# Preparation of the time-mixing operands placed beside the second half of the projection

## The reference, cut to what matters

```python
n = rms_norm(x, ln1_g)
proj = n @ w_in                          # 1024 -> 3072 columns
rkv = centred_conv(proj[..., :1536], conv_rkv)
r, k, v = split(rkv)                     # 512 each
# low-rank layer of the time mixing
delta = 0.5 * (shift_prev(n) + shift_next(n)) - n
g = sigmoid((n + delta * mix_g) @ gate_g1) @ gate_g2
kk = normalise(k * k_k)                  # per head of 64
for d in range(2):
    w = exp(-DECAY * sigmoid(decay_w0[d] + tanh((n + delta * mix_w[d]) @ decay_w1[d]) @ decay_w2[d]))
    a = sigmoid(aaa_a0[d] + ((n + delta * mix_a[d]) @ aaa_a1[d]) @ aaa_a2[d])
    kd = k * (1 + (a - 1) * k_a)
    y += wkv7_scan(r, w, kd, v, -kk, kk * a, reverse=(d == 1))
    bonus += sum(r * kd * r_k) * v
```

## Time and profile before

| | us |
|---|---|
| median of 3 runs | 2380.55 (2373.26 to 2381.06) |
| profiled execution, its own time | 2381.69 |
| its span, first to last instruction | 2379.9 |
| mean granted TensorE clock | 0.934 of full |
| TensorE busy | 2144.3 (90%) |
| VectorE busy | 1139.2 (48%) |
| ScalarE busy | 841.2 (35%) |
| GpSimd busy | 418.8 (18%) |

### The profile page before, as it was taken

The page is one execution under the profiler, slowest core; times in us unless marked ns, Lnnn a source line. Parts: engine busy times, 40 slices in busy tenths (PEclk is TensorE's granted clock), DMA queues, the critical chain, the costliest instruction groups (busy, mean ns, idle before and its releaser), DMA issues. The chain is left out here.

```text
span 2379.9 us, 41105 instructions
## 1 busy us (share of the span) xinstructions
PE 2144.3 (90%) x16892; PEld 1803.2 (76%) x16892; DVE 1139.2 (48%) x1613; ACT 841.2 (35%) x1445; POOL 418.8 (18%) x440
## 2 busy tenths in 40 slices
PE   6999999875567888778999799999999999999999
PEld 5887667643445555577886588999998899999887
DVE  5436553289685766655778543232333132323222
ACT  6213553366463444453454222222222122222211
POOL 0002331000006995064454000000000000000000
PEclk8999999867777999958999899999999999999999
DMA  4222111545871001048882644222233332222231
GB/s 159 95 88 81 41 61 61 188 182 218 297 208 57 1 1 54 12 121 183 188 185 71 200 140 147 88 71 79 71 102 94 122 115 79 72 78 71 80 124 67
DMA packets 134064, 258.96 MB, mean 109 GB/s; under 512 B 11200, under 2 KB 81216, under 8 KB 132512
## 3 DMA queue, kind: packets, MB, share of 16 engines
q1 hardware_dynamic: 133920, 256.93, 34.8%
HBM read 184.98 MB, written 68.93 MB: 107 GB/s over the span
## 5 line engine op out<-in xcount | busy, mean ns | idle before, releaser
L224 PE MATMUL ff_acc<-normed_nh,normed_ff_low 128*128 128x320 f32 x1344 | 416.5, 310 | 6.5 <-SPq L172 5.3
L225 PE MATMUL ff_acc<-normed_nl,normed_ff_high 128*128 128x320 f32 x1344 | 416.2, 310 | 0.0
L226 PE MATMUL ff_acc<-normed_nh,normed_ff_high 128*128 128x320 f32 x1344 | 416.1, 310 | 0.0
L2796 DVE TENSOR_TENSOR normed_ff_low<-normed_ff_raw,normed_ff_high 128x1024 fp32r<-128x1024 f32 x126 | 154.4, 1225 | 427.8 <-ACT normed_ff_high L2760 427.6
L224 PEld LDWEIGHTS ff_acc<-normed_nh,normed_ff_low 128*128 128x128 f32 x1344 | 253.2, 188 | 7.2 <-SPq L172 5.6
L225 PEld LDWEIGHTS ff_acc<-normed_nl,normed_ff_high 128*128 128x128 f32 x1344 | 253.2, 188 | 0.0
L226 PEld LDWEIGHTS ff_acc<-normed_nh,normed_ff_high 128*128 128x128 f32 x1344 | 253.2, 188 | 0.0
L2760 ACT CAST normed_ff_high<-normed_ff_raw 128x1024 fp32r<-128x1024 f32 x126 | 131.8, 1046 | 234.7 <-PE ff_acc L226 233.8
L225 PE MATMUL ff_acc<-normed_ff_low,ff_hh 128*128 128x512 f32 x420 | 163.4, 389 | 0.0
L224 PE MATMUL ff_acc<-normed_ff_high,ff_hl 128*128 128x512 f32 x420 | 163.4, 389 | 0.0
L226 PE MATMUL ff_acc<-normed_ff_high,ff_hh 128*128 128x512 f32 x420 | 163.4, 389 | 0.0
(11 more groups left out here) (343 smaller groups left out, 4377.8 us busy)
## 6 DMA issues: line engine op xcount, KB each, us to landing
ch_ops<-dram_sx SPq DMA_DIRECT2D x88, 256.0 KB, 5.3
normed_ff_raw<-in_w_gate SPq DMA_DIRECT2D x44, 512.0 KB, 3.5
normed_ff_raw<-in_w_up SPq DMA_DIRECT2D x44, 512.0 KB
normed_ff_raw<-in_w_down SPq DMA_DIRECT2D x44, 512.0 KB, 3.7
dram_sx<-pr_sx SPq DMA_DIRECT2D x7, 2816.0 KB, 8.1
pj_packed<-in_w_in SPq DMA_DIRECT2D x24, 512.0 KB, 4.6
heads_vt<-dram_sx SPq DMA_DIRECT2D x44, 256.0 KB, 4.9
dram_proj<-pj_mixed SPq DMA_DIRECT2D x12, 656.0 KB, 3.5
```

Of the source, the lines that this page charges most:

```text
L224: nc.tensor.matmul(out, ll, rh, start=start, stop=False)
L225: nc.tensor.matmul(out, lh, rl, start=False, stop=False)
L226: return nc.tensor.matmul(out, lh, rh, start=False, stop=stop)
L2796: nc.vector.tensor_tensor(low[s][:, :], raw[s], high[s][:, :].bitcast(F32), ALU.subtract).then_inc(cut_low[s], 1)
```

## The change

The two Blocks become one, norm_project_prep.

- The tiles of the projection come in another order (ORDER): k, r and v of f = 0, then of f = 1, and so on, then the attention's tiles.
- The 24 low-rank items stand behind pieces 6 to 31 (piece_of), beside the tiles that are convolved, where they stood behind pieces 36 to 62.
- From piece 36 on the projection uses three PSUM banks; the fourth and those of the low-rank layer go to the preparation.
- The preparation goes by 12 units (four f, three ranges of 512, 512 and 384 padded tokens), one each 2.75 pieces from piece 36: its first decays behind piece w0_at, the second ones and VectorE's whole unit at the next piece, the second exponentials at the one after.
- A unit's sx and bonus are stored, and the k, r and v of the unit three further on are loaded, from within SyncE's loop over the pieces. A tile's weights are loaded one tile earlier.
- The buffers of the preparation lie where those of the first half lay. So piece 33 brings a hand-over: hidg is stored, GpSimd waits for that and clears the padding, then the first loads are issued.
- The nine loads for the next Block go into the place of nh and nl, so they are issued only after the last piece.
- The next Block waits for the projection's stores itself.

```diff
-def norm_project_lora(nc, g):
+def norm_project_prep(nc, g):
+    ORDER = [n * FT + f for f in range(FT) for n in (1, 0, 2)] + list(range(CONV, MT))
-    BANKS = 4
+    BANKS, LATER_BANKS, CHANGE = 4, 3, PIECES // 2
-    chunk_of = lambda item: TN * CONV + item + item // KT
+    piece_of = lambda item: FIRST + item + item // KT
+    START, RATE = CHANGE, 2.75
+    w0_at = {START + int(RATE * u): u for u in range(NU)}
+    w1_at = {i + 1: u for i, u in w0_at.items()}
+    exp_at = {i + 2: u for i, u in w0_at.items()}
+    LOADS_AT = piece_of(ALL_ITEMS - 1) + 2
...
             @block.sync
+                load(2)
+                for i in range(PIECES):
+                    if i in finished:
+                        p = finished[i]
+                        if p + 3 < MT:
+                            load(p + 3)
+                        store(p)
+                    if i == LOADS_AT:
...
+                        sp.dma_start(g.hidg_dram[:, 0, :], hidg[:, 0, :]).then_inc(hidg_stored, 16)
+                        sp.dma_start(g.hidg_dram[0:GL - P, 1, :], hidg[0:GL - P, 1, :]).then_inc(hidg_stored, 16)
+                        sp.wait_ge(padded, 1)
...
+                        for u in range(len(SEGS)):
+                            load_kr(u)
+                            load_v(u)
+                    if i in exp_at:
+                        u = exp_at[i]
+                        store_sx(u, 0)
+                        if u:
+                            store_bonus(u - 1)
+                            if u + 2 < NU:
+                                load_v(u + 2)
+                        store_sx(u, 1)
+                        if u + 3 < NU:
+                            if UNITS_OF[u + 3][1] == 0:
+                                rows_stored(UNITS_OF[u + 3][0])
+                            load_kr(u + 3)
+                sp.wait_ge(done, PIECES)
+                for to, of in ((g.raw_first, g.proj[CONV * P:(CONV + 1) * P, :]), (g.cos_sb, g.cos), (g.sin_sb, g.sin),
+                               *((t, g.small_of(name)) for name, t in g.ahead_small.items())):
+                    sp.dma_start(to[:, :], of).then_inc(ahead_in, 16)
...
             @block.tensor
+                    if u or d:
+                        pe.wait_ge(sig_w, 2 * u + d)
+                        pe.wait_ge(sig_a, 2 * u + d)
+                    for ps, rows, sem in ((psw, HALVES[0], w_prod), (psa, HALVES[1], a_prod)):
+                        nc.tensor.matmul(span(ps, u), w2[rows, f, d, :], g.hid[rows, d, in_seg(u)], start=True, stop=True).then_inc(sem, 1)
...
+                    if i in w0_at:
+                        u = w0_at[i]
+                        decays(u, 0)
+                        if u == 0:
+                            pe.wait_ge(heads_in, 48)
+                            square_sums(0)
+                        else:
+                            bonus_of(u - 1)
+                    if i in w1_at:
+                        u = w1_at[i]
+                        decays(u, 1)
+                        spread_norms(u)
+                        if u + 1 < NU:
+                            square_sums(u + 1)
...
             @block.scalar
+                    if i in exp_at:
+                        u = exp_at[i]
+                        exponentials(u, 1)
+                        if u + 1 < NU:
+                            root_k(u + 1)
+                        if u + 2 < NU:
+                            square_k(u + 2)
+                        if u + 1 < NU:
+                            to_rows(u + 1)
+                    if i == START - 1:
+                        square_k(0)
+                    if i in w0_at:
+                        u = w0_at[i]
+                        sigmoids(u, 0)
...
+                    if i in w1_at:
+                        u = w1_at[i]
+                        sigmoids(u, 1)
+                        scale_a(u, 0)
+                        scale_a(u, 1)
+                        exponentials(u, 0)
...
             @block.vector
+                def unit(u):
+                    s = UNITS_OF[u][1]
+                    sums_of(u, 0)
+                    sums_of(u, 1)
+                    if u:
+                        bonus_of(u - 1)
+                    to_come(u)
+                    norm_k(u)
...
+                    if u + 1 < NU:
+                        floor(u + 1)
+                    operands(u, 0)
+                    if u + 1 < NU:
+                        invert_k(u + 1)
+                    operands(u, 1)
...
+                    if i in w1_at:
+                        unit(w1_at[i])
-def prep(nc, g):
...
@@ def solve_and_attention_in
                 sp.dma_start(heads[:, :], g.small_of("quarter_heads")).then_inc(small_in, 16)
+                for sem in g.proj_stored:
+                    sp.wait_ge(sem, g.proj_stores)
                 load_raw(1)
```

More of the change, by code:

```diff
@@ L258, in norm_project_lora @@
[L258 to L263, removed]
+        with Ctx(nc, "lo") as early:
+            own = early.sb("own", (P, 4, D))
+            lw, lwg = early.sb("w", (P, KT * 4 * HD)), early.sb("wg", (P, KT * GL))
+            less, half = (early.sb(n, (P, 5 * KT)) for n in ("less", "half"))
+            nk = [early.sb(f"nk{s}", (P, 514)) for s in range(2)]
+            near = [early.sb(f"near{s}", (P, 512)) for s in range(2)]
+            hidg = early.sb("hidg", (P, 2, PTOK))
+            partial, fold = early.sb("partial", (P, 512)), early.sb("fold", (P, BLK))
+            gate_mix = [early.sb(f"gate_mix{s}", (P, 512)) for s in range(4)]
+            ss, mean, rms, rstd = (early.sb(n, (P, TT)) for n in ("ss", "mean", "rms", "rstd"))
+            mixed = [early.sb(f"mixed{s}", (P, TOK)) for s in range(2)]
@@ new lines, in norm_project_prep @@
+        late = c.enter_context(Ctx(nc, "pr"))
+        slots = lambda name: [late.sb(f"{name}{s}", (P, 512)) for s in range(2)]
+        k, r, v = ([late.sb(f"{n}{s}", (P, hi - lo)) for s, (lo, hi) in enumerate(SEGS)] for n in ("k", "r", "v"))
+        w2, first = late.sb("w2", (P, FT, 2, P)), late.sb("first", (P, 512))
+        heads_rk, without_a = late.sb("heads_rk", (P, FT, P)), late.sb("without_a", (P, FT))
+        q, rows, kk, kds, bon = (late.sb(n, (P, 512)) for n in ("q", "rows", "kk", "kds", "bon"))
@@ new lines, in norm_project_prep @@
+        sg, av, cs, ex, kd = (slots(n) for n in ("sg", "av", "cs", "ex", "kd"))
+        tot, st = late.sb("tot", (P, 2, 512 // CH)), late.sb("st", (P, 2, 2 * 512 // P))
+        sx = [late.sb(f"sx{d}", (P, 512 // CH, 4, CH)) for d in range(2)]
+        with Ctx(nc, "parts") as parts:
+            g.nh, g.nl = (parts.sb(n, (P, KT, TT * P), F32R) for n in ("nh", "nl"))
+        g.lend_ahead(nc)
+        pair_mix = [own[:, :, :].rearrange("p s d -> p (s d)")[:, s * 512:(s + 1) * 512] for s in range(8)]
@@ new lines, in load_v, with rows_stored @@
+                def load_v(u):
+                    f, s = UNITS_OF[u]
+                    if f:
+                        sp.wait_ge(bonus, u - len(SEGS) + 1)
+                    row = (2 * FT + f) * P
+                    for at, token, n_tok in runs_of[s]:
+                        sp.dma_start(v[s][:, at:at + n_tok], g.proj[row:row + P, token:token + n_tok]).then_inc(v_in[s], 16)
+                def rows_stored(f):
+                    for p in range(3 * f + 1, 3 * f + 3):
+                        sp.wait_ge(stored[p % 2], 16 * (p // 2 + 1))
@@ L458, in _ @@
                 turn(10)
-                for i in range(3, len(SEQUENCE)):
+                for i in range(3, PIECES):
                     product(i)
@@ L2864, in __init__, with lend_ahead @@
         self.keep = dram["keep"]
+    def lend_ahead(self, nc):
+        self.ahead = Ctx(nc, "ahead")
+        self.raw_first, self.cos_sb, self.sin_sb = (self.ahead.far(n, (P, TOK)) for n in ("raw", "cos", "sin"))
+        self.v_rows = [self.ahead.far(f"v{s}", (P, FT, 6 * CH)) for s in range(2)]
+        self.ahead_small = {n: self.ahead.far(n, (P, SCOLS[n][1])) for n in ("quarter_mean", "ident", "swap", "centre")}
     def small_of(self, name):
```

775 lines of the change are left out of this document (327 added, 448 removed).

## The result

The changed kernel takes 2299.85 us (median of 4 runs, 2295.49 to 2306.47) against 2378.68 us for the kernel before on the same chip: a ratio of 0.9674 with a 95% interval of 0.964 to 0.9709, 78.8 us less. The forecast was 2305 us. The profiled execution took 2295.61 us (span 2293.8, mean granted clock 0.958), 86.1 us less than the one before it (2381.69). Each trace is one execution.

The account below looks back on a forecast made before the run. TensorE bounds the projection, VectorE the preparation. 60 + 8 + 8 = 76 us more TensorE time, then 30 us from the last piece, bring the next Block's first rotated tile 77 us earlier: 2381.7 - 77.1, say 2305 us; range 2285 to 2345.

Parts of the forecast that it names:

- TensorE's work for the units: Beside pieces 36 to 71: decay products, bonus products, sums of squares and norm spreading add 60 us, bounds 55 and 84.
- Couplings: Waits between queues in the units' stretch and at the hand-over: 8 us, between 2 and 25.
- first rival: In the units' stretch ScalarE's and VectorE's queues set the pace: 2352 us, milder form 2335; chance 15%.
- inside 19.1: Longest loop between queues, sigmoid to VectorE's unit to sigmoid, takes 14.3 us, within TensorE's 19.1 us a unit.
- hand-over at piece 35: Waits for hidg's stores, GpSimd's zeros and k's load: some 20 us after piece 32, where three pieces give 14.
- Low-rank move: Low-rank items moved to pieces 6 to 31: VectorE covers them thinly, 8 us, between 0 and 25.
- second rival: In the first half VectorE cannot keep up, 25 us in place of 8: 2322 us; chance 12%.
- Last piece to mark: From the last projected piece into the next Block, loads ahead no longer hidden: 30 us, bounds 25 and 40.
- Table switches: Some 36 loads of 1.28 us in the units; rival, a switch holds ScalarE longer than its load: 2319 us, 2%.
- Hidden anyway: Rival: the next Block, DMA share 0.98, gives back what its earlier start gains, at most some 20 us: 2325; 4%.
- slower: Rival: sigmoid, VectorE's unit, sigmoid run serially with TensorE's pieces, 28.7 us a unit: 2420 us; chance 6%.
- the mark: First finished rotated tile of the next Block (L1827): at 632.3 us before, forecast at 555.2, 77 us less.

Follow-up runs that it names:

- rate_3: The changed kernel with 3 pieces between all units in place of 2.75: 2298.92 us, ratio 0.968 to the kernel before.
- bonus_twice: The changed kernel with each bonus matmul issued twice into the same bank: 2310.53 us, ratio 0.9709 to the kernel before.
- act and dve kernels: The changed kernel with three or nine more ScalarE copies a unit, or four more VectorE products a unit: 2304.84, 2324.35 and 2302.72 us.
- ahead_early: The changed kernel with 2.5 pieces between units, nh and nl in their own memory, next Block's loads issued once the last unit's streams are stored: 2291.69 us.
- ahead_even: The changed kernel with next Block's loads issued early, nh and nl in their own memory, short gaps behind the narrow units: 2288.27 us.
- units_after: The changed kernel with all 12 units behind the last projected piece, loads ahead issued right behind that piece: 2409.64 us, ratio 1.0119 to the kernel before.
- items_alone: The kernel before with only the low-rank items moved to where the change puts them: 2391.5 us, ratio 1.0047 to the kernel before.
- rate_25: The changed kernel with 2.5 pieces between the units in place of 2.75: 2308.43 us, ratio 0.9693 to the kernel before.
- even_gaps: The changed kernel with the three gaps of two pieces moved behind the three narrow units: 2300.5 us, ratio 0.9684 to the kernel before.
- dve_plus_4: The changed kernel with four more VectorE products of 128x384 at the head of each unit: 2302.72 us, ratio 0.9682 to the kernel before.
- act_plus_9: The changed kernel with nine more ScalarE copies of 128x384 a unit: 2324.35 us, ratio 0.9769 to the kernel before.

## Why the prediction was right

- **TensorE's work for the units, 60 us forecast.** rate_3, in which TensorE never stops, needs 230.9 - 173.3 = 57.6 us for it (the last unit's bonus product comes behind the last piece). The pair of half-row decays does overlap as taken (two groups of 25 us side by side for the 24 forecast).
- **Couplings, 8 us (2 to 25).** The stops are 5.6 us, without loss of clock in this kernel. bonus_twice and the act and dve kernels speak against the first rival as a pace: 18.5 and 26.7 us of queue work cost 6.0 and 5.8. But the slack is thinner than "inside 19.1" says: 55.4 us on ScalarE cost 26.4, and a closer rate 14.4. The hand-over at piece 35, which the forecast feared, shows no stop: TensorE first waits at 308.4. The prediction named the right wait (sigmoid banks where units stand two pieces apart, 1 to 2 us) and left out that a stop can lower the clock.
- **Low-rank move, 8 us (0 to 25).** 6.5 measured, 6.0 by the clock time of piece 35. But of the reason given, VectorE falling behind the mixes while GpSimd works, only the 1.3 us stop is there; 2.9 us vanish with another place for nh and nl, in ahead_early and ahead_even. The term was right in size and partly wrong in cause. The second rival (25 us) is out. Its bound was also worked out wrongly: 5.4 us more in a tile with 3.4 us of room are 2.0 us over, not 7.4, and ten such tiles 20 us, not 74.
- **A term missing: the pieces' own pace.** The forecast took 4.70 us a piece from the earlier trace rows for the changed kernel too. It is 4.81 there (5.62, 5.62 and 3.20 for three): **b** of units_after is 173.3 for 169.0 in items_alone, so 4.3 us of the 66.9 that the stretch grew are neither units nor couplings. The three parts, 57.6, 5.6 and 4.3, make 67.5 against the 66.9 measured and 68 forecast. So the last piece came within 3.1 us partly by luck: this term stood at nothing, and the three others were 2.4, 2.4 and 1.5 us too high.
- **Last piece to mark, 30 us (25 to 40).** 27.7: the next Block begins 8.9 us after the last copy (10 forecast), the loads have landed after 13.3 (14), and 14.3 remain (16). ahead_early shows that the landing was worth what it was taken for.
- **Table switches.** 36 loads of 1.28 us, as forecast, and again no drain shows: a load begins 0.02 us behind the instruction before it, and the next one 0.01 us behind the load. So the rival stays rejected here.

```profile
384.35 0.63 ACT L740 ACTIVATE pr_ex<-pr_ex 128x512 f32<-128x512 f32 x1
385.00 1.28 ACT L712 ACT_TABLE_LOAD   x1
386.29 0.21 ACT L712 ACTIVATE pr_st<-pr_st 128x6 f32<-128x6 f32 x1
```

  The Trainium skill (ScalarE: Activation LUTs, What ACT_TABLE_LOAD costs) has a drain of 1.38 us on top of each load. The trace disagrees. That the kernel ran at TensorE's pace would not have shown it: 36 such drains, by that page's figure an estimated 50 us, would still fit into the 57 us of the 235.9 in which ScalarE stands idle.
- **Hidden anyway, slower.** The 82.5 us at the mark reach the end, as 86.1; from the mark to the end the traces of all the kernels take 1740 to 1753 us, so the 3.6 are no gain of their own. A unit alone takes 15.4 us where 14.3 was read off, far from the 25.5 at which the serial case decides.

By the profiled execution the sum (2304.6) is 9.0 us too high: 5.4 at the mark, 3.6 behind it. The 5.4 are 3.1 by the last piece and 2.3 behind it, both inside their bounds. Two slips change nothing: by the bounds as stated (55, 0, 2 and 25; 84, 25, 25 and 40) the ends are 2281 and 2373 and not 2285 and 2370, and ScalarE's slope by the two copies of the earlier trace rows is 0.80 ns a column and not 0.83.

## What to carry to other kernels

Work that VectorE and ScalarE bound and that stands by itself is best put beside a stage that TensorE bounds. Its price is then TensorE's share of it: here 58 us, with 10 us of stops and slower pieces and 6.5 us for the items moved, for 155 us less behind the last piece, though the same units by themselves made the kernel slower than before. Place such units by the tightest hand-over and not by a mean rate: units 2.5 instead of 2.75 pieces apart made the stretch 14 us longer, and one short gap before the wrong narrow piece 3 us. And when buffers are moved to make room, measure the bounding engine's own pace again.

## What was not expected of the hardware

- **The pace of a matmul depended on where its operands lay.** At full granted clock, 100% busy and with no wait, a wide piece of 24 matmuls takes 5.44 to 5.49 us in the kernel before, items_alone, ahead_early and ahead_even, and 5.62 in every kernel that has nh and nl behind the preparation's buffers. It is not the number of banks: piece 34, still with four, takes 5.62 us in units_after and 5.44 in items_alone, and ahead_early is fast with three. rate_25 and ahead_early differ in those buffers' places and in the loads ahead, and it is the faster one that has the loads beside its last pieces. So I hold the place to be the likely cause; whether it is the address's alignment (a tile of four words a row lies before nh) or the part of the memory stays open, and was not tried.
- **A stop of 2.8 us sometimes halved the clock and sometimes not.** Before each of them TensorE had run at 2.4 GHz, without another stop of over 0.3 us, for more than 30 us. In rate_25 (twice), even_gaps, ahead_early (twice), ahead_even and dve_plus_4 the granted clock then stood at 0.50 for 5 us or more. In the changed kernel the same stop, ending at 390.0, left it at 1.00, in both executions profiled:

```profile
385.00:390.00 5.00, 2.23 (x17) 2.01 (x16) 2.65 (x6) 4.96 (x8) 0.00 (x0) 1.00 0.87 308
390.00:395.00 5.00, 4.98 (x29) 4.00 (x30) 3.86 (x5) 4.97 (x9) 0.00 (x0) 1.00 1.01 331
```

  In dve_plus_4 the stop is of the same 2.79 us in the same unit, and the clock fell; in bonus_twice it fell to 0.66 behind one of only 1.93 us. In act_plus_9 it fell behind stops of 2.29 to 5.80 us. What tells these apart no run here shows, nor whether the same kernel does the same each time. A fall is worth 3 to 5 us, as much as most of the edits tried.
